# A decoder layer with a 32-expert mixture on one core: an earlier input piece, a reordered value stage, a split last expert, and cache copies in 6,144-byte packets

## What is computed

```python
def _attn_step(q, k_new, v_new, cache_k, cache_v, rel_bias):
    wb = cache_k.shape[1]
    kcat = jnp.concatenate([cache_k, k_new], axis=1)
    vcat = jnp.concatenate([cache_v, v_new], axis=1)
...
    return _merge_dilations(outs, lses), kcat[:, -wb:], vcat[:, -wb:]
```

## Time and profile before

| | |
|---|---|
| median of 3 runs | 1586.22 us |
| profiled execution | 1590.57 us, span 1588.7 us |
| TensorE, VectorE, ScalarE, GpSimd busy | 79%, 32%, 12%, 4% of the span |
| DMA | 608.83 MB, mean 383 GB/s; SP's queue 479.10 MB, ACT's 100.73, GpSimd's 28.37 |
| mean granted TensorE clock | 0.918 |
| chain that ended last | DMA 50%, TensorE 43%, VectorE 3% |

### The profile page before, as it was taken

The page is one execution under the profiler, slowest core; times in us unless marked ns, Lnnn a source line. Parts: engine busy times, 40 slices in busy tenths (PEclk is TensorE's granted clock), DMA queues, the critical chain, the costliest instruction groups (busy, mean ns, idle before and its releaser), DMA issues.

```text
span 1588.7 us, 23505 instructions
## 1 busy us (share of the span) xinstructions
PE 1260.9 (79%) x10063; PEld 654.6 (41%) x10063; DVE 501.4 (32%) x1042; ACT 193.5 (12%) x464; POOL 59.6 (4%) x111
## 2 busy tenths in 40 slices
PE   7969999998999989676777677677677676676675
PEld 4434458773887866322222222222222222222222
DVE  2300155740000342442332332332332332332333
ACT  3200012320111134100000000000000000000000
POOL 2000012212000000000000000000000000000000
PEclk9989999997899999899889899899898998999898
DMA  9999999979899885699999999999999999999996
GB/s 358 339 370 332 331 348 375 390 226 366 308 395 407 333 339 216 285 398 426 425 427 428 424 428 426 424 427 427 424 428 428 423 429 426 424 429 426 426 427 259
DMA packets 113181, 608.83 MB, mean 383 GB/s; under 512 B 11118, under 2 KB 14341, under 8 KB 78681
## 3 DMA queue, kind: packets, MB, share of 16 engines
q1 hardware_dynamic: 71243, 479.10, 73.1%
q10 hardware_dynamic: 34486, 100.73, 17.4%
q0 software_dynamic: 7408, 28.37, 5.0%
HBM read 603.16 MB, written 106.18 MB: 446 GB/s over the span
## 4 chain that ended last, share of the span: by engine, by line
DMA 50%; PE 43%; DVE 3%; issue 2%; SPq 1%; ACT 1%; POOL 0%; DVEq 0%; ACTq 0%
DMA ring<-in_w_e_up_dram 44%; PE pb L1108 11%; PE pb L642 10%; PE pb L881 6%; DMA ring<-in_w_in_dram 3%; PE pb L728 2%; PE pb L1008 2%; PE pb L899 2%; PE pb L670 2%; DMA ring<-in_w_cq_dram 2%; PE pb L849 1%; PE pb L648 1%; DMA ring<-Z 1%; SPq L486 1%; PE pb L859 1%
## 5 line engine op out<-in xcount | busy, mean ns | idle before, releaser
L1108 PE MATMUL pb<-ring,xT 128*32 128x256 f32 x4096 | 312.4, 473 | 198.6 <-DMA ring<-in_w_e_up_dram 197.8
L1108 PEld LDWEIGHTS pb<-ring,xT 128*32 128x32 f32 x4096 | 155.2, 134 | 378.9 <-DMA ring<-in_w_e_up_dram 245.4
L1948 DVE TENSOR_TENSOR Z<-pb,Z 128x512 f32<-128x512 f32 x256 | 158.4, 680 | 343.8 <-PE pb L1072 343.8
L642 PE MATMUL pb<-ring,hreg 128*128 128x512 f32 (+1 forms) x320 | 127.4, 558 | 13.9 <-issue 13.9
L1135 PE MATMUL pb<-ring,xT 128*32 128x512 f32 x992 | 113.9, 600 | 0.0
L1072 PE MATMUL pb<-xT 32*128 32x512 f32 (+1 forms) x768 | 106.2, 623 | 3.7 <-DVE Z L1948 2.6
L1048 PE MATMUL pb<-Z,xT 128*32 128x512 f32 (+1 forms) x768 | 95.3, 610 | 3.0 <-DVE xT L1926 3.0
L642 PEld LDWEIGHTS pb<-ring,hreg 128*128 128x128 f32 x320 | 61.1, 193 | 77.1 <-issue 75.4
L881 PE MATMUL pb<-hreg,ring 128*128 128x264 f32 x320 | 78.1, 402 | 2.8 <-DMA ring<-in_w_out_dram 2.8
L728 PE MATMUL pb<-hreg,ring 128*128 128x264 f32 x320 | 76.2, 398 | 5.1 <-DMA ring<-in_w_in_dram 5.1
L1450 ACT ACTIVATE xT<-pb 128x128 f32<-128x128 f32 x32 | 8.9, 277 | 526.8 <-PE pb L1108 526.8
(11 more groups left out here) (323 smaller groups left out, 1122.6 us busy)
## 6 DMA issues: line engine op xcount, KB each, us to landing
ring<-in_w_e_gate_dram SPq DMA_DIRECT2D x64, 2048.0 KB, 19.0
ring<-in_w_e_up_dram SPq DMA_DIRECT2D x64, 2048.0 KB, 23.5
ring<-in_w_e_down_dram SPq DMA_DIRECT2D x31, 4096.0 KB, 22.1
out_win_k_sample_dram<-in_cache_win_k_dram ACTq DMA_DIRECT2D x24, 1536.0 KB, 12.9
out_win_v_sample_dram<-in_cache_win_v_dram ACTq DMA_DIRECT2D x24, 1536.0 KB, 14.9
ring<-in_w_in_dram SPq DMA_DIRECT2D x7, 4096.0 KB, 30.8
ring<-in_w_out_dram SPq DMA_DIRECT2D x4, 4096.0 KB, 32.1
out_win_k_sample_dram<-in_cache_win_k_dram ACTq DMA_DIRECT2D x8, 1488.0 KB, 14.9
```

The lines of the kernel that those rows point to most:

```text
L642: last = mm(bk[:, 0:n], xt[:, k, tile * P:tile * P + P], w[:, k, 0:n], start=(k == 0), stop=(k == KT - 1))
L1108: last = mm(pb[1][32 * c:32 * c + 32, 0:256], XT[:, k % 4, 32 * (k // 4):32 * (k // 4) + 32], w[:, :, k8, P * c:P * c + P], start=(k == 0) ...
L1948: last = V.tensor_tensor(d, banks[c][:, :], d, ALU.add)
```

## The change

- SP issues the first w_in piece ahead of the bias bounce instead of behind it.
- TensorE does the state matmuls ahead of `channels(9)`, the first value group right behind it and ahead of `channel_rows(8, 10)`; the wait for the pool map weights comes after that. The ten maps stand before value groups 1 to 7 (two before groups 3, 4 and 6) instead of behind all groups. VectorE waits for the channel rows of tiles 8 and 9 before it changes their sample columns.
- The branch on n_over comes ahead of the last expert on TensorE, ACT and VectorE. Without overflow the last expert's second gate/up half comes in four DMAs and its down matrix in four, by halves of the output columns and pairs of row blocks. The results of the two column halves are combined, added and stored apart (`last_down`, `results`), and the samples are stored from ACT.
- A copy part moves its rows in runs of two, 6,144 bytes; the last part of each cache leaves 31 single rows to a second DMA instead of 15. Five of the 64 parts are issued later: one fewer each behind the memory keys, at w_in pieces 1 and 2, at `channels(9)` and in the maps, and five more from the cross-attention's queries to its output projection.

```diff
+            big(IN0)
             sp.wait_ge(v_freed, v_at("bias", 0))
             sp.dma_start(bias_dram[:, :], brow[0:H, :]).then_inc(brow_stored, 16)
...
-            big(IN0)
             big(IN0 + 1)
...
+            sp.wait_ge(dn_used, NE - 1)
+            w = a["w_e_down"][0][NE - 1].rearrange("(k p) n -> p k n", p=P)
+            for q in range(4):
+                c, f = slice(1024 * (q // 2), 1024 * (q // 2) + 1024), slice(2 * (q % 2), 2 * (q % 2) + 2)
+                sp.dma_start(slot2.rearrange("p (k n) -> p k n", k=4)[:, f, c], w[:, f, c]).then_inc(last_landed[q], 16)
...
-            channels(9)
-            channel_rows(8, 10)
-
...
-            piece_landed(pe, POOLW)
             pe.wait_ge(state_landed, 16)
             bk = vbank("state")
...
+            channels(9)
...
+            pe.wait_ge(a_freed, a_at("sturn", 1))
+            sample_values(0)
+            channel_rows(8, 10)
+            piece_landed(pe, POOLW)
+            kt = 0
+            for b in range(1, NB):
+                for _ in range(2 if b in (3, 4, 6) else 1):
+                    pool_map(kt)
+                    kt += 1
+                sample_values(b)
...
+            def last_down(hf, fs, bank):
+                for f in fs:
+                    for c in (2 * hf, 2 * hf + 1):
+                        last = mm(bank[32 * c:32 * c + 32, :], aT[:, 32 * f:32 * f + 32],
+                                  slot2[:, D * f + 512 * c:D * f + 512 * c + 512], start=(f == 0), stop=(f == 3))
+                return last
...
+                expert(NE - 1, last_of_all=True)
+                pe.wait_ge(last_landed[0], LAST_LANDED[0])
+                last_down(0, (0, 1), pb[3])
+                pe.wait_ge(last_landed[1], LAST_LANDED[1])
+                last_down(0, (2, 3), pb[3]).then_inc(dn_used, 1)
+                pe.wait_ge(gt_ready, NE)
+                pe.wait_ge(last_landed[2], LAST_LANDED[2])
+                last_down(1, (0, 1), pb[2])
+                pe.wait_ge(y_added, 3 * (NE - 1))
+                pe.wait_ge(yo_ready, NE)
+                results(0)
+                pe.wait_ge(last_landed[3], LAST_LANDED[3])
+                last_down(1, (2, 3), pb[2]).then_inc(dn_used, 1)
+                pe.wait_ge(yo_ready, NE + 1)
+                results(1)
...
-                        act.dma_start(dst[2032:WB - 1], src[2032:WB - 1]).then_inc(copied, 16)
-                    r = slice(512 * q, 512 * q + 512 if q < 3 else 2032)
-                    act.dma_start(dst[r].rearrange("(j e) n -> e j n", e=16), src[r].rearrange("(j e) n -> e j n", e=16))\
-                        .then_inc(copied, 16)
+                        act.dma_start(dst[2016:WB - 1], src[2016:WB - 1]).then_inc(copied, 16)
+                    r = slice(512 * q, 512 * q + 512 if q < 3 else 2016)
+                    act.dma_start(dst[r].rearrange("(j e t) n -> e j (t n)", e=16, t=2),
+                                  src[r].rearrange("(j e t) n -> e j (t n)", e=16, t=2)).then_inc(copied, 16)
...
+                if j == 8:
+                    dve.wait_ge(a_filled, a_at("uout", 3))
```

More of the change, by code:

```diff
@@ L355, in hybrid_decoder_layer @@
         yo_ready, y_filled, y_added = sem("yo_ready"), sem("y_filled"), sem("y_added")
-        x_final = sem("x_final")
+        x_final, out_filled = sem("x_final"), sem("out_filled")
+        last_landed = [sem(f"last_landed{i}") for i in range(3)] + [dn_landed]
+        quarter_landed = sem("quarter_landed")
+        LAST_LANDED = [16, 16, 16, 16 * (NE - 1)]
         cdr = a["const"]
@@ L851, in pool_map, with sample_values @@
                 last.then_inc(a_filled, 1)
-            pe.wait_ge(a_freed, a_at("sturn", 1))
             sv = vbank("svals")
-            for b in range(NB):
+            def sample_values(b):
                 val_ready(pe, b)
@@ L1082, in combine_in_turn, with results @@
                 combine(blocks, t)
[L1084 to L1094, removed]
+            def results(hf):
+                for t in ((0, 1), (0, 2, 1))[hf]:
+                    if t == 2:
+                        pe.wait_ge(x_final, 1)
+                    for c in range(4) if t == 2 else (2 * hf, 2 * hf + 1):
+                        r = slice(32 * c, 32 * c + 32)
+                        out = (pb[4 + c][:, :], pb[c][:, :], pb[4][32 * c:32 * c + NB, :])[t]
+                        last = mm(out, GT[r, slice(P * t, P * t + P) if t < 2 else slice(SEQ, TOK)], yo[r, :], start=True, stop=True)
+                    last.then_inc(out_filled, 1)
+            def last_down(hf, fs, bank):
[4 more added lines that the diff above has]
+                return last
             def expert(i, last_of_all=False):
@@ L1112, in expert @@
                         combine_in_turn(i, half)
+                if last_of_all:
+                    combine(i, 2, pb[0:1])
                 pe.wait_ge(hid_ready, i + 1)
@@ L1456, in expert @@
                 nc.scalar.copy(GT, pb[2][:, 0:TOK]).then_inc(gt_ready, 1)
-                act.wait_ge(dn_used, i + 1)
-                nc.scalar.copy(yo, pb[3][:, :]).then_inc(yo_ready, 1)
+                if not last_of_all:
+                    block_out(i)
             rows_out(0)
@@ L1463, in _ @@
             n_over = act.value_load(ov_i[0:1, OVB:OVB + 1], min_val=0, max_val=OVB)
-            expert(NE - 1, last_of_all=True)
             with act.If(n_over > 0):
-                rows_out(NE)
-                with act.Fori(NE, NBLK) as i:
+                with act.Fori(NE - 1, NBLK) as i:
                     expert(i)
+            with act.Else():
+                expert(NE - 1, last_of_all=True)
+                act.wait_ge(dn_used, NE)
+                nc.scalar.copy(yo[0:64, :], pb[3][0:64, :]).then_inc(yo_ready, 1)
+                act.wait_ge(dn_used, NE + 1)
+                nc.scalar.copy(yo[64:P, :], pb[2][64:P, :]).then_inc(yo_ready, 1)
+            act.wait_ge(x_final, 4)
+            for c in range(4):
+                act.dma_start(a["y_sample"][:, 0, 512 * c:512 * c + 512], x3s[32 * c:32 * c + NB, :]).then_inc(stored, 16)
         @block.vector
@@ L1948, in add_results, with results @@
                     last = V.tensor_tensor(d, banks[c][:, :], d, ALU.add)
-                    if final and c == 1:
-                        last.then_inc(x_final, 1)
-                last.then_inc(x_final if final else y_added, 1)
+                last.then_inc(y_added, 1)
+            def results():
+                for n, (hf, t) in enumerate(((0, 0), (0, 1), (1, 0), (1, 2), (1, 1))):
+                    dve.wait_ge(out_filled, n + 1)
+                    if t == 2:
+                        last = V.tensor_tensor(x3s, pb[4][:, :], x3s, ALU.add)
+                    for c in (2 * hf, 2 * hf + 1) if t < 2 else ():
+                        d = x3[:, t, 512 * c:512 * c + 512]
+                        last = V.tensor_tensor(d, pb[c if t else 4 + c][:, :], d, ALU.add)
+                    last.then_inc(x_final, 1)
             def expert(i, last_of_all=False):
```

92 lines of the change are left out of this document (52 added, 40 removed).

## The result

The changed kernel takes 1578.51 us (median of 12 runs, 1572.66 to 1588.89) against 1590.01 us (1583.3 to 1601.98) for the kernel before beside it: a ratio of 0.9927, interval 0.9900 to 0.9954, some 11.6 us faster. The forecast was 34.3 us. Single executions more than 1.5% above the fastest of their kernel are left out of the ratios. A "±" behind a difference of two ratios is the root of the sum of the squares of their half intervals.

A forecast was written before the change was run, and what follows sets the result against it. TensorE bounds up to about 640 us, then DMA in the experts. Gains 15.9 + 13 + 7.6 less costs 2 and 0.2 give 34.3 us: 1590.57 to 1556.3 us, 1552 as a median; range 1536 to 1574.

The forecast's parts named there:

- D: Cache copies in two-row packets of 6,144 bytes: net cost 2 us, ends a gain of 4 and a cost of 12.
- Share: Copy packets beside weight pieces: the longer copy turn would cut a 4.19 MB piece from 167 to 104 GB/s while copies wait.
- A: First w_in piece issued ahead of the bias wait: the 13.88 us hole at 85.88 goes, 15.9 us gained, floor 12.
- At two pieces, 8 us each: Rival: copies hold back two weight pieces by 8 us each instead of the 2 us counted, 1566 us; chance 11%.
- Six pieces at 15 us each: Rival, slower: the longer copy turn binds at six w_in, w_out and w_cq pieces, 90 us, 1640 us; chance 5%.
- E: Five copy parts moved from the first 400 us to the cross-attention: only ScalarE issue cost, 0.2 us slower.
- DMA stays as full as it was: Moved copy parts: 19 us of DMA leave a stretch that the first two parts shorten by 30 us.
- B: State, sample values and pool maps reordered: waits and low clock go, 13 us gained, ends 3 and 17.
- clock term: State-and-maps stretch: 21 us at half clock would be some 11 at full clock, 10 us gained.
- The cap of the prediction: State and maps: the first w_out piece lands at 387.5, maps end at 402.17, so the gain is at most 14.7 us.
- What is late next: no price: Behind the early w_in piece: queued bias read needed some 60 us on, second piece has some 30 us, so no cost.
- C: Last expert and branch: last landing to end takes 10.8 us instead of 18.4, 7.6 us gained, ends 5 and 9.

The follow-up runs named there:

- f4: Changed kernel with copy packets of four rows, 12,288 bytes, instead of two; 0.9996 of the kernel before.
- f1: Kernel before with only the copy packets changed, to two rows (6,144 bytes); 1.0104 of the kernel before.
- f6: e4 with copy packets of half a row, 1,536 bytes; 0.9823 of the kernel before.
- e1: Changed kernel with the second w_in piece issued ahead of the bias read instead of behind it; 0.9922 of the kernel before.
- h1: Changed kernel with two-row packets only in the first 16 of 64 copy parts, one-row packets in the others; 0.9867 of the kernel before.
- g1: Changed kernel without the cache copies (100 MB left out) and without the wait for them at the end; 0.9659 of the kernel before.
- e3: Changed kernel with copy packets of one row, 3,072 bytes, again; 0.9833 of the kernel before.
- e4: Changed kernel with the second w_in piece ahead of the bias read and one-row copy packets; 0.9816 of the kernel before, 1554.59 us against 1583.85.
- h2: Changed kernel with one-row packets in the first 16 copy parts and two-row packets in the other 48; 0.9892 of the kernel before.
- f5: e4 with the five moved copy parts issued at their old places again; 0.9882 of the kernel before.
- kE: Kernel before with only the five copy parts moved to the cross-attention; 0.9935 of the kernel before.
- kB: Kernel before with only the new order of state, sample values and pool maps; 0.9993 of the kernel before.
- kA: Kernel before with only the early issue of the first w_in piece; 0.9923 of the kernel before.

## Why the prediction was wrong

**D failed, and by itself makes over half the miss.** "Share" had the mechanism right, and the prediction then put it aside: "They don't: ACT asks for 16.90 MB in 87 us, 194 GB/s, less than the 308 GB/s that the longer turn gives." That is a mean over a stretch in which the copies come in bursts. The rows to believe stood in its first paragraph: in the earlier trace rows the queues move equal packet counts, which in these traces goes with work waiting on both (where the copies have run out, in f4, it is 2453 to 106), and at the earlier trace rows the copies moved 245 GB/s, above that mean. In such a stretch a packet twice as long leaves a weight piece 98 GB/s (after) or 96 (f1) instead of 168. The first w_in piece shows it across executions, since every kernel with A and the copies issues it between 46.9 and 48.3 us, beside the same copy parts. From issue to landing it took 25.9 us beside half-row packets (f6), 31.1 to 35.9 beside one-row packets (seven kernels), 37.6 to 44.9 beside two-row packets (after, e1, h1) and 39.4 beside four-row packets (f4); without copies 13.9 (g1, issued at 42.81). The trade cannot be paid out of DMA time: the copies' share fell only from 17.4% of 1588.7 us to 17.1% of 1573.7, 276 to 269 us. Mis-sized term: +2 forecast, +15 to +17 measured in three comparisons (f1, e3, e1 to e4), each ± 8 or 9 us; the values, though not the whole of their intervals, lie beyond the term's upper end of 12; the doubled dose (f4) cost 11 us (± 7) more. The rivals held this mechanism. "At two pieces, 8 us each" even had the size, 16; its 1566 missed through the other terms, and the price is not confined to two pieces (h2). Six pieces at 15 us each did not come about; f4's second fence shows how a piece can get off more lightly, since copies served sooner also end sooner and it then has the engines almost alone. The Trainium skill, DMA: Bandwidth & Descriptors, Queues, rings and completion order, says that each DMA engine goes round its queues and drains a whole packet before it switches. The traces agree (769 to 768, 456 to 453).

**E failed in sign.** "DMA stays as full as it was" was nearly so (share 0.95 before and 0.90 after from 133 to 348 us, 0.98 and 0.95 from 403 to 520), and the wrong question. Moving the five parts gave 10 us in both comparisons. f5's fence shows one way, that the copies stand beside a piece TensorE waits for. kE's profile does not: its first projection starts 1.3 us later than before, and 10 us of its gain lie in the stretch from state to sel (42.91 us against 52.98, below), which varies by more than that between executions of one order. Where kE's gain arises stays open.

**B failed in size, at its clock term.** "At full clock these 21 us would be some 11: 10 lost" took one execution's 21 us at half clock as what the old order always loses and the new one gets back whole. The windows from state to sel, which in the new order hold channels(9) (7.4 us) as well, are, for the old order in before and in kE and for the new one in kB:

```profile
348.98:401.96 52.98, 46.35 (x243) 22.04 (x241) 5.87 (x16) 4.74 (x11) 13.92 (x25) 0.73 0.95 366
```

```profile
344.42:387.33 42.91, 38.48 (x243) 19.36 (x241) 5.87 (x16) 4.73 (x11) 13.91 (x25) 0.88 0.96 315
```

```profile
340.25:396.02 55.77, 51.35 (x276) 27.09 (x274) 11.39 (x26) 6.30 (x19) 11.00 (x21) 0.79 0.87 330
```

Six profiled executions of the old order range from 41.5 to 56.0 us (clock 0.70 to 0.88), thirteen of the new one from 45.1 to 55.8 (clock 0.79 in kB, 0.90 to 1.00 in the other twelve). So the new order does keep the clock higher, by less than forecast. With 7.4 us added to the old the means are 56.1 and 49.1: 7 us gained in place, not 13. And it does not all arrive: in kB the wait behind w_cq grew from 0.54 to 5.96 us, since that piece's landing follows DMA. The cap of the prediction looked at the first w_out piece alone, which in the changed kernel landed at 388.0, as worked out (387.5); the later ones and w_cq were late next.

**A: the first half right, "What is late next: no price" wrong.** The hole at 86 went, but with luck: the piece landed at 85.3 and not "near 81", and in h1, whose program and copies are the same up to there, it took 44.1 us and left a hole of 10.41, and in e1 one of 7.86. And the bias read moved from 59 to 86 us, onto the second piece, whose slack of "some 30 us" was used up: with this order and one-row packets there 5.21 (e3), 8.11 (kA) and 8.60 us (h2) were lost, with longer packets 14.85 (after) and 12.94 (f4), in h1 nothing. The term is 12 alone and 8 to 10 inside, for 15.9.

**C: right in kind.** From the last landing to the end it is 13.0 us against 10.8 worked out, so the tail gained 5.4 us for 7.6: the last part's eight matmuls start 2.7 us after it lands, behind the first half's combine, and the 16 combine matmuls took 3.18 us instead of 0.6 for four. Fewer VectorE adds stand behind them (two instead of five), which gives 1.8 back.

Terms A, B, C and E alone would have given 26 us (e3), not 36. A part of the remaining difference is not resolved: the terms by themselves sum to 19.2, the whole is 11.6, and each term is known only to ± 4 to 9 us.

## What to carry to other kernels

Take equal packet counts of two queues in a window as a sign that both are backlogged there, and ask the share question in that window and not over a mean. Where a large copy runs beside weights that an engine waits for, do not lengthen the copy's packets for their efficiency (here 3,072 bytes were better than 6,144, and 1,536 brought nothing more), and place its parts where no piece is due. A stall or a low clock seen in one profiled execution is not a term until another execution shows it, and when a transfer is moved forward, list what is queued behind it and where that lands now.

## What was not expected of the hardware

A DMA issue can hold its engine: in f6 one copy issue on ScalarE took 15.97 us and TensorE waited 11.70 us for it. From 540 to 562 us the copies, 836 packets beside 836 of the expert weights, moved only 57 GB/s, so they had a backlog; with one-row packets (e4) the longest such issue there was 9.36 us at 549.59. In the changed kernel, with two-row packets, no copy issue from 440 us on took over 0.61 us. And copy packets of 1,536 bytes cost the DMA engines only 6% more time than packets of 3,072.
